# Conformer's last two chunks, its LayerNorm and four output slots, and the final norm, by token halves

## What is computed

```python
def conformer_conv_module(h, w_pw1, b_pw1, w_dw, b_dw, ln_g, ln_b, w_pw2, b_pw2):
    a, g = jnp.split(h @ w_pw1 + b_pw1, 2, axis=-1)
    u = a * jax.nn.sigmoid(g)
    u = causal_depthwise_conv(u, w_dw) + b_dw          # 31 taps
    u = jax.nn.silu(layer_norm(u, ln_g, ln_b))
    return u @ w_pw2 + b_pw2

def first_block(x, ...):                               # layer 1 of 2
    m = conformer_conv_module(rms_norm(h, norm_mix_pre[1]), ...)
    h = h + rms_norm(m, norm_mix_post[1])
    h = h + rms_norm(swiglu_ffn(rms_norm(h, norm_ffn_pre[1]), ...), norm_ffn_post[1])

def second_block(x, ...):
    h = h + conv_ffn(rms_norm_2(h, ffn_norm[layer]), ...)
    return rms_norm_2(h, final_norm)
```

## Time and profile before

| | us |
|---|---|
| median of 3 runs | 2391.07 (2390.69 to 2394.46) |
| the profiled execution | 2390.31, span 2388.3 |
| PE busy in the span | 2312.5 |
| DVE busy, ACT busy | 1331.1, 876.0 |
| granted PE clock, mean of the span | 0.989 |

### The profile page before, as it was taken

How to read it: one execution, slowest core, us unless ns; L and a number is a source line. 1 busy time by engine, 2 the same in 40 slices (tenths; PEclk the granted TensorE clock), 3 DMA queues, 4 the chain that set the end, 5 groups by cost and what they waited for, 6 DMA issues and landing times.

```text
span 2388.3 us, 35719 instructions
## 1 busy us (share of the span) xinstructions
PE 2312.5 (97%) x13818; PEld 1942.5 (81%) x13818; DVE 1331.1 (56%) x1927; ACT 876.0 (37%) x1332; POOL 8.4 (0%) x8
## 2 busy tenths in 40 slices
PE   8999999999997999999999999999999989999997
PEld 6878888889876888888988877888888778888886
DVE  6564745432757564542366575666633885766523
ACT  6444422222524532222342364333322573333322
POOL 0000000000000000000000000000000000000000
PEclk9999999999998999999999999999999999999999
DMA  4212232322374232222232112222233102222232
GB/s 151 69 59 78 85 124 97 97 97 89 99 178 87 71 106 97 97 97 97 89 104 81 56 62 71 97 97 97 97 97 97 65 27 90 96 97 97 97 97 79
DMA packets 81576, 218.64 MB, mean 92 GB/s; under 512 B 10944, under 2 KB 29760, under 8 KB 81472
## 3 DMA queue, kind: packets, MB, share of 16 engines
q1 hardware_dynamic: 77680, 216.10, 28.7%
q10 hardware_dynamic: 3792, 1.05, 0.2%
HBM read 212.78 MB, written 4.34 MB: 91 GB/s over the span
## 4 chain that ended last, share of the span: by engine, by line
PE 83%; DVE 9%; ACT 4%; issue 2%; DMA 1%; SPq 0%; DVEq 0%; ACTq 0%
PE bank L461 25%; PE bank L463 24%; PE bank L462 24%; PE bank L657 2%; PE bank L656 2%; PE bank L658 2%; DVE w_lo L1565 1%; ACT ds L1517 1%; ACT w_hi L1059 1%; DVE acc L1594 1%; PE bank L784 1%; DVE small L2218 1%; DVE m L1621 1%; DVE ds L2237 1%; DVE h L1626 1%
## 5 line engine op out<-in xcount | busy, mean ns | idle before, releaser
L461 PE MATMUL bank<-u_hi,w_hi 128*128 128x512 f32 (+1 forms) x2088 | 798.9, 383 | 14.0 <-issue 8.6
L1059 ACT ACTIVATE w_hi<-raw 128x1024 fp32r<-128x1024 f32 x378 | 400.3, 1059 | 1087.0 <-PE bank L463 977.2
L462 PE MATMUL bank<-u_lo,w_hi 128*128 128x512 f32 (+1 forms) x2088 | 789.1, 378 | 0.0
L463 PE MATMUL bank<-u_hi,w_lo 128*128 128x512 f32 (+1 forms) x2088 | 788.8, 378 | 0.0
L1565 DVE TENSOR_TENSOR w_lo<-raw,w_hi 128x1024 fp32r<-128x1024 f32 x378 | 461.4, 1221 | 407.0 <-ACT w_hi L1059 406.5
L461 PEld LDWEIGHTS bank<-u_hi,w_hi 128*128 128x128 f32 x2088 | 396.0, 190 | 92.7 <-issue 12.3
L463 PEld LDWEIGHTS bank<-u_hi,w_lo 128*128 128x128 f32 x2088 | 395.9, 190 | 72.8
L462 PEld LDWEIGHTS bank<-u_lo,w_hi 128*128 128x128 f32 x2088 | 396.2, 190 | 71.6 <-issue 1.2
L461 PE MATMUL bank<-hid_hi,w_hi 128*128 (+1 forms) x528 | 208.0, 394 | 0.0
L463 PE MATMUL bank<-hid_hi,w_lo 128*128 (+1 forms) x528 | 207.0, 392 | 0.0
L462 PE MATMUL bank<-hid_lo,w_hi 128*128 (+1 forms) x528 | 204.9, 388 | 0.0
(11 more groups left out here) (295 smaller groups left out, 2501.4 us busy)
## 6 DMA issues: line engine op xcount, KB each, us to landing
raw<-weights_dram SPq DMA_DIRECT2D x378, 512.0 KB, 3.5
bz<-gated_dram SPq DMA_DIRECT2D x32, 268.0 KB, 5.5
gated_dram<-bz SPq DMA_DIRECT2D x8, 274.0 KB, 2.6
h<-x_t_dram SPq DMA_DIRECT2D x8, 256.0 KB, 6.3
out_dram<-m SPq DMA_DIRECT2D x8, 256.0 KB, 2.2
cmask<-masks_dram ACTq DMA_DIRECT2D x4, 224.0 KB, 3.8
ap<-select_dram SPq DMA_DIRECT2D x1, 512.0 KB, 8.9
bwv<-vectors_dram SPq DMA_DIRECT2D x4, 112.0 KB
```

The costliest lines, as they stand in the source:

```text
L461: pe.matmul(out, wh, xh, start=start, stop=False)
L462: pe.matmul(out, wh, xl, start=False, stop=False)
L463: return pe.matmul(out, wl, xh, start=False, stop=stop)
L1059: act.activation(w_hi[:, j, :], raw[:, j, :], ACT.Copy).then_inc(hi_ready, 1)
```

## The change

- Conformer: chunks 6 and 7 run by token halves. `piece` numbers six whole chunks and four half pieces (6 and 7 in the first half, then in the second). Slots 12 to 15 of `b_in` run their first half, then their second; `gated`, `shift_gated`, `depthwise`, `spread`, `shifted` and the squares follow by pieces of 64 phase columns.
- LayerNorm by halves: `norm_sums` adds sum and squares of the two last chunks as ones products; `layer_root` and `silu_pair` on ACT, `layer_norm` on DVE work on 256 tokens, two chunks at a time. `by_lo` now shares the memory of `u_lo`.
- Slots 0 to 3 of `b_out` run their first half (`first_outs(0)`), with the last spreads and convolution between, and then their second. Slots 0 to 2 of them are loaded and split during the last parts of `b_in`, slot 4 and on behind the second halves (`ahead` is RING there, not AHEAD).
- Ones products into an unused bank (`keep_awake`): 18 at the start of the kernel, 8 ahead of the first slot of the feed-forward of layers a and b, 18 ahead of `first_outs(1)`.
- Start: slot 0 runs alone instead of woven with slot 1; ACT and DVE split slot 0, all chunks of `h`, then slots 1 and 2. The first gains are loaded from ACT's queue.
- Final norm by halves: the second eleven slots of `d_ffn_out` run as 256-column products, the last four of them half by half; sum (`final_sums`), root, multiplications (all on DVE) and stores (SP and ACT in turn, two chunks each) are made for each half. POOL has no part in it now.

```diff
+WHOLE = KC - 2
+PIECES = WHOLE + 4
...
+def piece(p):
+    if p < WHOLE:
+        return p, None
+    return WHOLE + p % 2, (p - WHOLE) // 2
+def phase_columns(half):
+    return (0, COLS) if half is None else (COLS // 2 * half, COLS // 2)
...
+    return items + [
+        ("part", 0), ("part", 1), ("gated", 6), ("conv", 4), ("spread", 3),
+        ("part", 2), ("part", 3), ("gated", 7), ("conv", 5), ("spread", 4),
+        ("part", 4), ("part", 5), ("gated", 8), ("conv", 6), ("spread", 5), ("conv", 7), ("spread", 6),
+        ("part", 6), ("spread", 7), ("part", 7), ("gated", 9),
+    ]
...
+            def shift_gated(p):
+                c, half = piece(p)
+                at, n = phase_columns(half)
                 b = c % CONV_RING
-                sp.wait_ge(bz_ready, c + 1)
-                sp.dma_start(gated_dram[b].rearrange("g (c r) j -> (g c) r j", r=PHASES), bz[:, c % 2, :, :]).then_inc(bz_kept, 16)
-                sp.wait_ge(bz_kept, 16 * (c + 1))
-                if c >= CONV_RING:
+                lo, hi = 0 if not half else LEAD // PHASES + at, LONG if half != 0 else LEAD // PHASES + n + 1
+                sp.wait_ge(bz_ready, p + 1)
+                if half:
+                    sp.wait_ge(bz4_landed[b], LANDED * (c // CONV_RING + 1))
+                sp.dma_start(gated_dram[b].rearrange("g (c r) j -> (g c) r j", r=PHASES)[:, :, lo:hi], bz[:, c % 2, :, lo:hi])\
+                  .then_inc(bz_kept, 16)
+                sp.wait_ge(bz_kept, 16 * (p + 1))
+                if half:
+                    sp.wait_ge(conv_full, TILES * (p - 2 + 1))
+                elif c >= CONV_RING:
                     sp.wait_ge(conv_full, TILES * (c - CONV_RING + 1))
+                n += REACH - COLS
                 for a in range(LAGS):
-                    of = gated_dram[b].rearrange("g m j -> m g j")[:, :, a:a + REACH]
-                    sp.dma_start(bz4[32 * a:32 * a + 32, b, :, :], of).then_inc(bz4_landed[b], 16)
+                    of = gated_dram[b].rearrange("g m j -> m g j")[:, :, a + at:a + at + n]
+                    sp.dma_start(bz4[32 * a:32 * a + 32, b, :, at:at + n], of).then_inc(bz4_landed[b], 16)
...
+            last = first + RING + 2 * WHOLE
+            shift_gated(WHOLE)
+            shift_gated(WHOLE + 1)
+            load_next(last)
+            load_next(last + 1)
+            shift_gated(WHOLE + 2)
+            load_next(last + 2)
+            load_next(last + 3)
+            shift_gated(WHOLE + 3)
...
+            def keep_awake(out, times):
+                for _ in range(times):
+                    pe.matmul(out[:, 0:P], ones[:, :], ones[:, :], start=True, stop=True)
...
+            def final_sums(half):
+                to = stat_bank("final", half)[:, tokens(half)]
+                pe.wait_ge(acc_ready, ACC["final"] + 3 + 3 * (half + 1))
+                pe.matmul(to, ones[:, :], acc[:, tokens(half)], start=True, stop=False)
+                pe.wait_ge(sq_ready, SQ["final"] + 4 + 2 * (half + 1))
+                pe.matmul(to, ones[:, :], sq[:, 1, HT:T], start=False, stop=True).then_inc(sum_full, 1)
...
+                            if n == 0 and "f" not in stat:
+                                keep_awake(bank[0], 8)
...
+                    if half and l == "d":
+                        for n in range(HALF - 4):
+                            back_halved(n, (0, 1))
+                        for part in range(2):
+                            for n in range(HALF - 4, HALF):
+                                back_halved(n, (part,), (lambda: final_sums(0)) if part and n == HALF - 3 else None)
+                        continue
...
-            two_chunks(0, bank[0:2], u_hi, u_lo, normed_input("a_pre"), high_input("a_pre"))
-            for n in range(2, 8):
+            keep_awake(bank[7], 18)
+            for n in range(8):
                 if n >= 4:
                     pe.wait_ge(qk_evac, n - 3)
-                chunk(n, 0, bank[n % 4][:, :], u_hi, u_lo)
+                chunk(n, 0, bank[n % 4][:, :], u_hi, u_lo, ready=normed_input("a_pre") if n == 0 else None)
                 if n == 2:
...
+            def norm_sums(half):
+                t, p = tokens(half), WHOLE + 2 * half
...
+                pe.wait_ge(b_squares, WHOLE - 1)
+                pe.matmul(square, ones[:, :], acc[:, t], start=True, stop=False)
+                pe.wait_ge(sq_ready, SQ["b_var"] + p + 1)
+                pe.matmul(square, ones[:, :], sq[:, 0, t], start=False, stop=False)
+                pe.wait_ge(sq_ready, SQ["b_var"] + p + 2)
+                pe.matmul(square, ones[:, :], sq[:, 1, t], start=False, stop=True).then_inc(var_full, 1)
+            def first_outs(half, between):
+                s, t = SLOT["b_out"], tokens(half)
+                pe.wait_ge(w_ready, s + 3)
+                for k in range(KC):
+                    if k % 2 == 0:
+                        pe.wait_ge(u_ready, SPLIT["b_ln"] + PAIRS * half + k // 2 + 1)
+                    for n in range(3):
+                        j = (s + n) % RING
+                        last = product(bank[n][:, t], weight(w_hi, j, k), weight(w_lo, j, k), by_hi[:, k, t], by_lo[:, k, t],
+                                       k == 0, k == KC - 1)
+                        if half and k == KC - 1:
+                            last.then_inc(slot_done, 1)
+                    if k % 2:
+                        between(k // 2)
+                last = half_chunk(s + 3, half, bank[3][:, t], by_hi, by_lo)
+                if half:
+                    last.then_inc(slot_done, 1)
...
+                elif what == "part":
+                    half, at = n // 4, n % 4
+                    pe.wait_ge(b_evac, 2 * WHOLE + (at + 1 if half else at - 3))
+                    half_chunk(SLOT["b_in"] + 2 * WHOLE + at, half, bank[at][:, tokens(half)], u_hi, u_lo)\
+                        .then_inc(slot_done if half else part_full, 1)
...
+            def last_pieces(pair):
+                if pair == 0:
+                    spread(WHOLE + 2)
+                elif pair == 2:
+                    depthwise(WHOLE + 3)
+                elif pair == 3:
+                    spread(WHOLE + 3)
...
+            norm_sums(0)
+            depthwise(WHOLE + 2)
+            pe.wait_ge(b_evac, 2 * PIECES)
+            first_outs(0, last_pieces)
+            norm_sums(1)
+            keep_awake(bank[6], 18)
+            first_outs(1, lambda pair: None)
+            halved_out("b_post", "b_out", by_hi, by_lo)
...
+            def slot_free(s):
+                act.wait_ge(slot_done, s + 1)
+                high_part(s + RING)
...
+            def layer_root(half):
+                t = tokens(half)
+                log_table()
+                act.wait_ge(mean_full, half + 1)
+                act.activation(bshift[:, t], STAT[:, t], ACT.Square, scale=1.0 / D).then_inc(msq_ready, 1)
+                act.activation(bmean[:, t], STAT[:, t], ACT.Copy, scale=1.0 / D).then_inc(mean_ready, 1)
+                act.wait_ge(var_ready, half + 1)
+                act.activation(rs[:, t], bvar[:, t], ACT.Ln, bias=eps[:, 1:2]).then_inc(rs_ln, 1)
+                act.wait_ge(rs_ln, RS["b_var"] + half + 1)
+                act.activation(rs[:, t], rs[:, t], ACT.Exp, scale=-0.5).then_inc(rs_ready, 1)
+                act.preload_act_table_set("silu_and_others")
...
+            def silu_pair(half, pair):
+                act.wait_ge(yn_ready, PAIRS * half + pair + 1)
+                for to, done in ((by_hi, uh_ready), (by, ut_ready)):
+                    for c in (2 * pair, 2 * pair + 1):
+                        ins = act.activation(to[:, c, tokens(half)], by[:, c, tokens(half)], ACT.Silu,
+                                             bias=col("ln_b", c), scale=col("ln_g", c))
+                    ins.then_inc(done, 1)
...
+                    elif n == WHOLE + 2:
+                        slot_free(SLOT["b_in"] + 2 * WHOLE)
+                        slot_free(SLOT["b_in"] + 2 * WHOLE + 1)
+                    elif n == WHOLE + 3:
+                        slot_free(SLOT["b_in"] + 2 * WHOLE + 2)
...
+            layer_root(0)
+            keep_piece(WHOLE + 2)
+            for pair in range(PAIRS):
+                silu_pair(0, pair)
+                if pair == 1:
+                    slot_free(SLOT["b_in"] + 2 * WHOLE + 3)
+            keep_piece(WHOLE + 3)
+            square_made(WHOLE + 2)
+            square_made(WHOLE + 3)
+            layer_root(1)
...
+                elif what == "part":
+                    half, at = n // 4, n % 4
+                    slot, t = SLOT["b_in"] + 2 * WHOLE + at, tokens(half)
+                    if half:
+                        dve.wait_ge(slot_done, slot + 1)
+                    else:
+                        dve.wait_ge(part_full, at + 1)
+                        dve.wait_ge(bz_ready, WHOLE - 1 + at // 2)
+                    dve.tensor_tensor(ba[:, at // 2, at % 2, t], bank[at][:, t], rs[:, t], ALU.mult).then_inc(b_evac, 1)
+                    if n == 1:
```

(63 more changed lines are left out.)

323 lines of the change are left out of this document (151 added, 172 removed).

## The result

The changed kernel takes 2399.26 us (median), the kernel before 2392.10 in the same comparison: ratio 1.0027, 95% interval 1.0018 to 1.0036. It is slower, by 6.4 us at the middle of the interval; the prediction was 2389.1 us, a range up to 2396.5, and 0.14 for slower.

The account below looks back on a forecast made before the run. The prediction took PE as the bound, busy 97% of the span. Its terms, start -3.2, boundaries -4.7, final norm -3.5 and Conformer's end +9.4, summed to -2.0 us: 2389.1 us against the median, range 2381 to 2396.5.

Parts of the forecast that it names:

- the two boundaries: Behind the output projections of fox mixer and Conformer: ones products win back the lost clock, gain 4.7 us (bounds 0 and 4.7).
- the Conformer's end: Slot 12 of `b_in` to slot 3 of `b_out`: new waits make it 91.8 us against 82.4, loss 9.4 (bounds 4 and 17).
- the gain of the start: Kernel start: slot 0 alone and earlier splits let slot 1 end earlier, gain 3.2 us (range 3.2 to 4.6).
- The first three parts: Start, two boundaries and final norm together: gains of 3.2, 4.7 and 3.5 us, 11.4 in all.
- The LayerNorm terms: First product of a pair waits for four SiLUs (1.7 us) and one subtraction (0.65) instead of one of 0.8: 1.4 more.
- Final norm: Kernel's end: 9.3 us behind the last product instead of 15.1, less 2.3 for halved slots: gain 3.5 (bounds 2 and 4.5).
- B: Conformer's new holes keep the clock, changes of kind cost nothing, start and tail give more: 2383 us; chance 0.33.
- C: Conformer's weight loads queue behind shifted-window reads, 7.2 us instead of 3.6: slower, 2396.2 us; chance 0.11.
- D: Ones products don't hold the clock at the two boundaries, +4.7 us: 2393.8 us; chance 0.06.
- E: Each half convolution and half `spread` takes as long as a whole one, +7.6 us: 2396.7 us; chance 0.05.

Follow-up runs that it names:

- reorder: The changed kernel with the split of the weights of `b_out` slots 0 and 1 moved behind the square and shift for `spread` 6 on ACT and DVE: ratio 1.0013.
- three_swap: The kernel before with new start, boundaries and final norm, old Conformer's end, and ACT's copy for the first `spread` ahead of the weight split: 2381.2 us, ratio 0.9956.

## Why the prediction was wrong, step by step

The measured 2399.26 us lies above the range. Three terms of the sum failed: the two boundaries (3.2 us), the Conformer's end (3.0) and the gain of the start, carried to the end as it was (2.5).

**Right in kind, and near in size.** The Conformer's halves are a loss by new waits on late weights. The first three parts were forecast at -11.4 and gave -7.0 at their places. The stretch from slot 12 of `b_in` to the start of slot 4 of `b_out` was forecast at 91.8 us and took 93.1 (707.75 to 800.88): waits 19.9 us, the ones products in them counted, for 17.4, work 73.3 for 74.4. The holes by themselves: 4.3 forecast and 5.6 found before `spread` 6 (the second load took from its issue, 733.3 at the latest, to 737.8: at least 4.5 us instead of 3.6), 5.3 and 5.6, 5.3 and 6.0 (780.59 to 786.61), 2.5 and 2.6. The 2.96 us in front of the half convolution's last product, which the forecast didn't have, are hidden in the first hole; they are what `reorder` couldn't win. The LayerNorm terms in the forecast (1.7 and 0.65 for 0.8) add up to 1.55, not 1.4.

**A step that failed: the start's gain was carried to the end.** I carried the start's 3.2 us unchanged to the end ("everything behind, by the same time" was said of the loss and taken for the gains too). It was 2.7 at its place; at the first LayerNorm sum, 650 us later, 1.0 was left of start and first boundary together, and the runs with and without the start show no difference at the end. The earlier trace rows held the clue, ACT's split of 653.93 after 5.28 us of waiting for its load; I used that row for a load time and did not ask which PE work stands behind such a split. What the runs show in its place: PE waits in the early Conformer until a weight load lands, and three_swap, which takes the copy out from behind that load, shortens the stretch by 6.7 us. Cost against the sum: 0.5 at the start and 2.0 in the early Conformer.

**A term that was mis-sized: the boundaries.** 4.7 forecast, 1.5 found. The clock held, as said (1.00 instead of 0.68 and 0.52); but time at 1.2 GHz is only lost where nothing else sets the pace. DVE's `u_lo` and `w_lo` do, as soon as PE is fast. I priced the whole 4.7 us, named no next limit there, and tied my lower bound, 0, to the clock falling all the same. That is 3.2 us, the largest miss.

**The Conformer's end**: 9.4 forecast, 12.4 found (bounds 4 to 17): 1.3 up to the start of slot 4 and 1.7 of lower clock behind slot 4 (5.2 us at 0.67), for which the sum had no term, since I counted clock for two holes and there were three with a fall behind them.

**Final norm**: 3.5 forecast, 2.8 found; 10.1 us behind the last product's start instead of 9.3. (The steps listed for it add up to 6.05 us, not the 6.6 that the sum uses; in the trace the last multiplication ends 7.1 us behind that start, and the stores take 3.1 more instead of 2.7.) Between these, 0.6 us of small gains. Together -2.0 + 0.5 + 2.0 + 3.2 + 3.0 + 0.7 - 0.6 = +6.8.

**Rivals.** B fell: low clock followed the three unfilled holes. C's delay of single loads was seen in small (0.9 us or a little more), not its 6.8. D fell: the clock held. E fell: 96 matmuls of 64 columns take 1.38 us (732.86 to 734.24), 14.4 ns each, the 14.5 that halving needs. The Trainium skill, "TensorE: Matmul & The Clock Gate" (section "Wait — 56ns, not 53.3ns?"), would have 2.4 us for them, an estimate; this trace disagrees. A half `spread` is not quite half a whole one: 0.66 us (748.39 to 749.05) instead of 0.52, some 0.6 us over four of them.

The range ended at 2396.5 because the rivals stood alone: none let a gain be absorbed, and the unfavourable bounds of the terms (0 for the boundaries, 17 for the Conformer's end) weren't added up.

## What to carry to other kernels

A gain far from the end is only worth what is left of it behind the next wait that isn't PE's: before you add it to the sum, look for the next hole of PE downstream and ask whether its releaser would come earlier as well. Read a short operation on which PE hangs together with what stands in front of it on its engine: a copy of 0.6 us behind the split of a weight that nobody needs yet cost this kernel 0.26%, with the lower clock behind its hole; no part of the change gave as much. Where a trace of one execution shows a few microseconds more in one stretch, compare the granted clock of both before you look for a cause. Where low clock is won back, name the engine that sets the pace at full clock first.
